# Two down projections by seven block products, their token combinations on VectorE

## What is computed

```python
# block 1
up = conv(h @ w_up) + conv_b;  val, gate = split(up)
x = x + g2 * ((silu(gate) * val) @ w_down)
# block 2
a, g = split(h @ w_up);  a = dwconv3x3(a) + conv_b
x = ALPHA * x + g5 * ((gelu(a) * g) @ w_down)      # then a layer norm over the channels
```

## Time and profile before

| | |
|---|---|
| median of 3 runs | 2506.64 us (2503.1 to 2508.11) |
| profiled execution | 2507.51 us, of which the span of instructions is 2505.7 us |
| mean granted TensorE clock | 0.988 of full speed |
| TensorE busy | 2390.1 us, 95% of the span |
| VectorE, ScalarE, GpSimd busy | 1634.7, 1019.3, 561.4 us |
| 30 weight splits of the down projections, VectorE L1907 | 92.8 us, 3.093 each |
| loads of down weights | 60 of 704 KB |

### The profile page before, as it was taken

How to read it: one execution, slowest core, us unless ns; L and a number is a source line. 1 busy time by engine, 2 the same in 40 slices (tenths; PEclk the granted TensorE clock), 3 DMA queues, 4 the chain that set the end, 5 groups by cost and what they waited for, 6 DMA issues and landing times. The chain is left out here.

```text
span 2505.7 us, 38163 instructions
## 1 busy us (share of the span) xinstructions
PE 2390.1 (95%) x16353; PEld 1291.5 (52%) x16353; DVE 1634.7 (65%) x2158; ACT 1019.3 (41%) x1219; POOL 561.4 (22%) x296
## 2 busy tenths in 40 slices
PE   7989889999999999999999999988989999999997
PEld 3447664444444444444767776774434444444443
DVE  6788847565545554555477878786878877773343
ACT  5117417345454531323354545442344444441221
POOL 0010000057777711000000000000036766630000
PEclk9999999999999999999999999999999999999998
DMA  9117674121212144443200000003112121225342
GB/s 338 34 53 237 195 229 160 62 73 52 67 51 68 51 148 122 110 109 127 64 26 18 26 26 23 21 26 126 51 51 67 51 68 51 68 64 176 94 114 90
DMA packets 307687, 224.62 MB, mean 90 GB/s; under 512 B 11424, under 2 KB 298302, under 8 KB 306367
## 3 DMA queue, kind: packets, MB, share of 16 engines
q1 hardware_dynamic: 306646, 221.86, 29.3%
q10 hardware_dynamic: 873, 0.32, 0.1%
HBM read 199.61 MB, written 22.03 MB: 88 GB/s over the span
## 5 line engine op out<-in xcount | busy, mean ns | idle before, releaser
L200 PE MATMUL ps<-hT,arena 128*128 128x512 bf16 (+1 forms) x2592 | 552.4, 374 | 15.8 <-DVE arena L2185 5.9
L2118 PE MATMUL ps<-hT,arena 128*128 128x512 bf16 x2280 | 498.9, 379 | 0.3 <-DVE ps L2269 0.3
L1923 PE MATMUL ps<-arena 128*128 128x512 bf16 x2106 | 459.0, 380 | 2.5 <-DVE arena L1907 2.5
L200 PEld LDWEIGHTS ps<-hT,arena 128*128 128x128 bf16 x2592 | 252.7, 98 | 313.3 <-issue 20.3
L2118 PEld LDWEIGHTS ps<-hT,arena 128*128 128x128 bf16 x2280 | 223.0, 98 | 269.8 <-issue 1.3
L1923 PEld LDWEIGHTS ps<-arena 128*128 128x128 bf16 x2106 | 206.3, 98 | 251.8 <-DVE arena L1907 3.8
L2194 POOL TENSOR_TENSOR arena<-arena 128x2048 f32<-128x2048 f32 x2 | 12.6, 6282 | 1138.7 <-DVE arena L696 1138.7
L2407 DVE SCALAR_TENSOR_TENSOR xT<-ps,vec,xT 128x945 f32<-128x945 f32 (+2 forms) x176 | 215.1, 1222 | 31.9 <-ACT xT L2390 26.4
L1907 DVE TENSOR_TENSOR arena<-hT,arena 128x2816 bf16<-128x2816 f32 x30 | 92.8, 3093 | 181.8 <-ACT arena L1902 181.6
L2118 PE MATMUL ps<-xT,arena 128*128 128x512 bf16 x912 | 203.0, 379 | 0.0
L2185 POOL TENSOR_TENSOR arena<-arena 128x2048 bf16<-128x2048 f32 x38 | 156.4, 4115 | 100.6 <-ACT arena L2177 100.6
(11 more groups left out here) (454 smaller groups left out, 3291.8 us busy)
## 6 DMA issues: line engine op xcount, KB each, us to landing
xT<-ada_w_dram SPq DMA_DIRECT2D x24, 1024.0 KB, 5.9
arena<-w_up_dram SPq DMA_DIRECT2D x44, 512.0 KB, 5.1
arena<-ffn_up_dram SPq DMA_DIRECT2D x44, 512.0 KB, 5.2
hT<-w_down_dram SPq DMA_DIRECT2D x30, 704.0 KB, 7.6
hT<-ffn_down_dram SPq DMA_DIRECT2D x30, 704.0 KB, 7.0
arena<-w_in_dram SPq DMA_DIRECT2D x33, 512.0 KB, 4.1
xT<-w_mod_dram SPq DMA_DIRECT2D x16, 1024.0 KB, 6.2
arena<-w_mod_dram SPq DMA_DIRECT2D x8, 1024.0 KB, 19.4
```

What stands on the lines that cost most here:

```text
L200: last = pe.matmul(out, lhs(a, kt), rhs(b, kt, i), start=start and kt == 0 and (a, b) == (0, 0), stop=stop and kt == n_k - 1 and (a, b) == ...
L1923: last = pe.matmul(self.bank(u), self.part(u, a, kt), self.g[:, b, kt, cols], start=kt == 0 and (a, b) == (0, 0), stop=kt == FT - 1 and (a ...
L2118: last = pe.matmul(out, self.stationary(u, block, a, kt), moving(b, kt), start=start and kt == 0 and (a, b) == (0, 0), stop=kt == 3 and (a ...
```

## The change

```diff
-class DownByHalves:
+class DownProducts:
...
+    def dve(self, dve, also=lambda i: None):
+        self.read_count, self.updated = 0, {}
+        for i in range(2, len(self.JOBS)):
+            if i + 1 < len(self.JOBS):
+                self.split_lo(dve, i + 1)
+            if i == 2:
+                self.update(dve, 0)
+            self.update(dve, i - 1)
+            for step, product in ((2, 5), (4, 3), (6, 6), (18, 7), (21, 4)):
+                if i == step:
+                    self.operand_lo(dve, product)
+            if i == 3:
+                self.second_combination(dve)
+            if 7 <= i < 13:
+                self.third_combination(dve, range(2 * (i - 7), min(2 * (i - 7) + 2, HALF_K)))
+            if 11 <= i < 17:
+                self.fourth_combination(dve, range(2 * (i - 11), min(2 * (i - 11) + 2, HALF_K)))
+            also(i)
+        self.update(dve, len(self.JOBS) - 1)
...
+        for r in rows:
+            for h in range(2):
+                last = r == HALF_K - 1 and h == 1
+                f.link(dve.tensor_tensor(self.spare_half, self.b11[:, r, h, 0, :], self.b11[:, r, h, 1, :], ALU.add))
+                done = dve.tensor_tensor(self.t3_f32[:, r, h, :], self.x[:, r, h * HALF // 2:(h + 1) * HALF // 2], self.spare_half,
+                                         ALU.subtract)
...
+        dve.tensor_tensor(self.x, self.y, self.x, ALU.subtract).then_inc(self.f.apart_set, 1)
...
+            pool.tensor_tensor(self.raw[out], self.raw[a], self.raw[b], op).then_inc(f.summed, 1)
...
+            row = u - HALF_K
+            if row >= 0:
+                pool.wait_ge(self.done, row + 1)
...
+                    pool.tensor_tensor(value, value, self.b11[:, row, :, part, :], ALU.subtract).then_inc(self.combined, 1)
...
     def multiply(self, dve, u):
-        c = self.conv_of(u, 0)
-        dve.tensor_tensor(c, c, self.conv_of(u, 1), ALU.mult).then_inc(self.multiplied, 1)
+        c, gate = self.conv_of(u, 0), self.conv_of(u, 1)
+        dve.tensor_tensor(self.second_half(u), self.second_half(u), gate[:, HALF:T], ALU.mult)
+        dve.tensor_tensor(self.g_first[:, u, :], c[:, 0:HALF], gate[:, 0:HALF], ALU.mult).then_inc(self.multiplied, 1)
...
+            down.dve(dve, beside)
+            total(1, 7)
+            m_norm.dve_finish(dve, (0,))
+            short.lo(dve, 0)
...
+            pe.wait_ge(down.read, down.updates_until(last_job - 1))
+            turn(1, 0, range(7))
+            turn(1, 2, range(4))
+            pe.wait_ge(squared, 3)
+            turn(1, 1, range(7))
+            pe.wait_ge(down.read, down.updates_until(last_job))
```

More of the change, by code:

```diff
@@ L2513, in _ @@
                     f.load(sp, 1)
-            f.sync(sp, down)
-            down.sync(sp, context)
+            f.sync(sp, down, context)
+            sp.wait_ge(down.lo, down.job(4, 1) + 1)
+            short.load(sp, 2)
+            sp.wait_ge(c_norm.ready, KD)
+            sp.dma_start(ctx_dram, k.hT[:, :, :, 0:CTX]).then_inc(ctx_saved, 16)
+            short.load(sp, 3)
             sp.wait_ge(ctx_saved, 16)
             short.load(sp, 0)
-            sp.wait_ge(down.made, last_u)
+            sp.wait_ge(down.made, last_job)
             short.load(sp, 1)
-            sp.wait_ge(down.made, 2 * KD)
-            for n in range(2, len(parts)):
-                short.load(sp, n)
+            sp.wait_ge(down.made, len(down.JOBS))
             sp.dma_start(gate_raw, ins["w_in_2"].rearrange("o (k p) n -> p (o k) n", p=P)[:, :, O_SG + P:IN2])\
@@ L2604, in _ @@
                 pe.wait_ge(short.lo_done, n + 1)
-                pe.wait_ge(down.read, min(2 * n + 13, 2 * KD))
+                pe.wait_ge(down.read, down.updates_until(down.job(4, min(2 * n, 3))))
                 short_unit(n, 0, before)
@@ L2785, in _, with total @@
             f.dve(dve, down)
-            def total(u):
-                half, t = divmod(u, KD)
-                dve.wait_ge(down.read, u + 1)
-                m_norm.dve_total(dve, u, half * HALF, (half + 1) * HALF, t)
+            def total(half, t):
+                product = ((3, 7), (2, 4))[half][t // 4]
+                dve.wait_ge(down.read, down.updates_until(down.job(product, t % 4)))
+                m_norm.dve_total(dve, half * KD + t, half * HALF, (half + 1) * HALF, t)
             def centre_tiles(steps):
@@ L2799, in _, with beside @@
             m_norm.dve_gain(dve)
[L2800 to L2816 removed]
+            def beside(i):
+                if i == down.job(7, 2):
+                    for t in range(5):
+                        total(0, t)
+                if i == down.job(7, 3):
+                    total(0, 5)
+                    total(0, 6)
                     dve.wait_ge(ctx_turned, 1)
@@ L3892, in _ @@
             f.act(act, down)
-            for u in range(2, 2 * KD):
-                down.split_hi(act, u)
-                if KD < u <= KD + 4:
-                    spread(0, u - KD - 1)
+            down.act(act, lambda i: spread(0, i - down.job(4, 1)) if i >= down.job(4, 1) else None)
+            spread(0, 3)
             for t in range(4):
@@ L4029, in _ @@
                 step()
+        @block.gpsimd
+        def _(pool):
+            f.pool(pool, n_norm)
+            down.pool(pool)
 STAGES = [
```

651 lines of the change are left out of this document (391 added, 260 removed).

## The result

| | before | after |
|---|---|---|
| median | 2505.31 us (4 runs, 2503.1 to 2508.11) | 2547.9 us (4 runs, 2541.87 to 2552.81) |
| profiled execution, its span | 2507.51, 2505.7 us | 2541.87, 2540.1 us |
| granted clock | 0.988 | 0.982 |

The ratio is 1.0161, with an interval of 1.0148 to 1.0175: 40 us slower by the ratio, 42.6 by the two medians. The forecast was 2563 us, in a range of 2525 to 2588. The profiled execution after is the fastest of its four, so the spans differ by 34.4 us only. What follows divides those 34.4.

The account below looks back on a forecast made before the run. The down projections were taken as bound by TensorE's matmuls, fewer paying only while VectorE keeps up. Matmuls -57.0, starts 26.4, middle 61.6 and the rest 25.4 gave +56.4 us, so 2563 us, range 2525 to 2588.

Parts of the forecast that it names:

- VectorE and GpSimd exclude each other: Operations with two SBUF inputs: one engine waits for the other's whole instruction, so GpSimd's weight sums hold VectorE up.
- Starts: Jobs 0 to 6 of both down projections: TensorE stalls before jobs 4, 5 and 6, 11.9 and 14.5 us, +26.4.
- middle: Jobs up to operand 7 in both down projections: VectorE's queue plus GpSimd sums exceed the matmuls, 30.8 us each, +61.6.
- last jobs: Jobs 19 to 27, first down projection: waits for the context's total plus transposes, means and sums of squares, 15.1 us.
- second stage, transposes and wait: Second down projection: half of the 64 row transposes, which take 8.2 us, and their wait, 4.2 us.
- behind the first stage: After the first down projection TensorE idles while the first half of the tokens is scaled and split, +16.5 us.
- tail: After the second down projection's last update: four reductions over 1024 elements and more transposes replace three short operations, +5 us.
- up projections: GpSimd's two new subtractions cost nothing; a multiply in two instructions costs +0.8 us, for the second stage's first units alone.
- 41.6 us of them hold VectorE up: Middle of each down projection: 13 of 16 GpSimd sums delay VectorE, making 123.4 us against 92.6 of matmuls.
- waits for the context's totals: Last jobs, first down projection: about 7.6 us before job (4,0), GpSimd's mask building getting in, and 1.9 at (4,3).
- the last part of the forecast: Signs in the profile: 256-element VectorE operations sometimes at 3.5 us instead of 0.41, TensorE gaps released by VectorE's split.

Follow-up runs that it names:

- e4: The changed kernel with the scaling of the first 512 tokens behind the first down projection cut to 8 tokens per VectorE operation: 2543.7 us.

## Why the prediction was right

The main reason held: VectorE and GpSimd exclude each other, and TensorE waits for VectorE's splits. It is shown from several sides (sums away, sums moved, sums cut up). The sizes were less good, and their errors partly cancel. Starts, middle and last jobs were put 37 us too high, and 15 us of matmuls at low clock were not in the sum. That the total came within 15 us of the median is in part luck. The sizes, term by term, in the profiled execution:

| term | forecast | measured |
|---|---|---|
| starts, both stages | +26.4 | 13.8 (6.3 and 7.5) |
| middle, gaps | +61.6 | 44.3 (23.0 and 21.3) |
| middle, low clock | not priced | 11.4 (3.1 and 8.3) |
| last jobs, stage one | 15.1 | 7.8 (5.2 of matmuls, 2.62 of wait), and 1.7 at low clock |
| second stage, transposes and wait | 4.2 | 4.1 |
| behind the first stage | +16.5 | 17.05, and 1.7 at low clock |
| tail | +5 | 4.6 |
| up projections | +0.8 | 0 in the first, -0.4 in the second |

By stages: the first +9.5 (forecast +23.7), behind it +17.1 (+16.5), the second +4.1 (+10.4), the tail +4.6 (+5), the up projections -0.4 (+0.8), together 34.9. Outside of these the two executions differ by +2.6 us before the first up projection and by -3.1 between the short convolution and the second one, low clock included. No run explains these two. That makes the 34.4.

- **Starts.** The term was twice too large. I had put a GpSimd sum of 3.2 us into VectorE's list before job 4. It was issued at 930.58 beside an operand part, waited, and ran mostly while VectorE updated from PSUM. The residual was there after 18.1 us, not 20.5. In the second stage the last tile was ready after 14.0 us, not 17, and the residual after 19.2, not 23. The other two gaps were put at 2.5 each and are 3.15 and 2.15.
- **Middle.** The price of a sum was right (3.15 to 3.2 us undisturbed). "41.6 us of them hold VectorE up" was too much: VectorE's operations were longer by 39 us over the whole stage with all 16 sums. A sum that lies beside an update or beside a wait for ScalarE costs nothing. The forecast had named this and set it off fully against waits.
- **Low clock.** The forecast priced gaps as idle time alone. The slow jobs add 11.4 us in the middle, 1.7 in the last jobs and 1.7 behind the first stage. TensorE's busy time agrees: 264 matmuls fewer are 57.0 us at full clock, and it fell by 42.6. These 15 us made up for a part of the two terms above.
- **Last jobs.** The waits for the context's totals were put at 9.5 us and are 2.62. The mask building hardly gets in: VectorE's additions of 256 elements took 0.44 us on the mean.
- **Behind the first stage** and the **tail** came out as worked out from the earlier trace rows.
- **Up projections.** In the first block it is 344.68 us in both kernels from the first matmul of the seven products' line to the down projection. In the second, where the 0.8 was put, it is 344.91 before and 344.47 after. So GpSimd's two new subtractions were hidden.
- The 256-element operations beside running sums took 3.26 us, as the last part of the forecast asked for, and the releaser was mostly VectorE's split. TensorE's idle time, put at 45 to 52 us a stage, was 31.9 and 29.3. No gap of TensorE in the two stages has a load as its releaser. VectorE itself waited 0.52 and 1.76 us for the residual before job 4, as the forecast had it, and e4, which had made VectorE faster, met a load behind the stage.

## What to carry to other kernels

When two engines exclude each other, work handed from the busy one to the idle one can cost the busy one the idle one's time. Compare the two durations (here 1.62 and 3.2 us, of which 2.4 were paid on the mean) before handing over, and if it must stay, cut it into short instructions. A saving of matmuls is worth what the engines that feed them have to spare. Price it for each stage alone. As it was made, the change paid in neither block. With the sums on VectorE and its list evened out, the second block alone gained 9.6 us. The first block's stage became 8.4 us shorter too, but the stage behind it had lost its cover and stood for 17.1 us.

## What the runs showed of the hardware

- **Who gets in.** GpSimd went ahead when VectorE left a gap, however short, or ran an update from PSUM. Chained operations, which wait for each other, leave 0.04 us. Operations without such a wait start before the last one's end, and keep GpSimd out over several. Timeline of the first sum:

```profile
929.59 6.02 DVE L2544 TENSOR_TENSOR arena<-arena 128x5632 bf16<-128x5632 f32 x1
...
930.58 9.59 POOL L2661 TENSOR_TENSOR hT<-hT 128x1408 f32<-128x1408 f32 x1 [42.70 <-DMA hT<-w_down_dram]
935.52 1.62 DVE L2518 TENSOR_TENSOR arena<-hT,arena 128x1408 bf16<-128x1408 f32 x1
...
937.06 2.06 DVE L2595 SCALAR_TENSOR_TENSOR xT<-ps,mod,xT 128x512 f32<-128x512 f32 x3
939.04 7.02 DVE L2565 TENSOR_TENSOR arena<-arena 128x5632 f32<-128x5632 f32 x1
```

```profile
2325.00:2452.00 127.00, 105.27 (x444) 45.06 (x445) 117.33 (x106) 27.78 (x16) 53.19 (x14) 0.92 0.44 120
```
